# Attention: scores one pair earlier, two heads per VectorE step, and the softmax sums as a diagonal operand of a matrix product

## The reference

```
k_all = concat([k, k_ctx]); v_all = concat([v, v_ctx])       # 256 + 256 keys
s = einsum('bqkgd,bskd->bkgqs', q, k_all) * HEAD_DIM**-0.5   # 8 heads of 64
p = softmax(s, axis=-1)
o = einsum('bkgqs,bskd->bqkgd', p, v_all)
```

## Time and profile before

| | us |
|---|---|
| median of 3 runs | 3051.02 (3049.09 to 3054.16) |
| the profiled execution | 3051.58 |
| its span, first to last instruction | 3049.9 |
| TensorE busy | 2901.1 (95%) |
| VectorE busy | 1690.8 (55%) |
| ScalarE busy | 1332.0 (44%) |
| GpSimd busy | 204.1 (7%) |
| mean granted TensorE clock | 0.981 of full speed |

### The profile page before, as it was taken

The page is one execution under the profiler, slowest core; times in us unless marked ns, Lnnn a source line. Parts: engine busy times, 40 slices in busy tenths (PEclk is TensorE's granted clock), DMA queues, the critical chain, the costliest instruction groups (busy, mean ns, idle before and its releaser), DMA issues. The chain is left out here.

```text
span 3049.9 us, 49455 instructions
## 1 busy us (share of the span) xinstructions
PE 2901.1 (95%) x18122; PEld 2565.0 (84%) x18122; DVE 1690.8 (55%) x2279; ACT 1332.0 (44%) x1862; POOL 204.1 (7%) x224
## 2 busy tenths in 40 slices
PE   6999999889999999999987998899999999998998
PEld 5878887667888878888877998899999999998998
DVE  6444326646454244442276547875557486659864
ACT  5333315344343133432245445554645345545553
POOL 1000001200000000000020001300300000003100
PEclk7999999899999999999999999999999999999999
DMA  6444324113454225442233553355535556553454
GB/s 217 160 151 166 117 96 154 63 42 125 151 165 145 97 70 171 158 138 97 93 102 116 185 192 131 118 170 195 178 121 191 193 175 214 195 172 104 162 196 132
DMA packets 120490, 443.60 MB, mean 145 GB/s; under 512 B 13568, under 2 KB 14976, under 8 KB 119744
## 3 DMA queue, kind: packets, MB, share of 16 engines
q1 hardware_dynamic: 119376, 431.38, 42.7%
q0 software_dynamic: 1008, 10.75, 0.9%
HBM read 441.03 MB, written 1.05 MB: 145 GB/s over the span
## 5 line engine op out<-in xcount | busy, mean ns | idle before, releaser
L1497 DVE TENSOR_TENSOR wlo<-raw,whi 128x1024 fp32r<-128x1024 f32 x816 | 1001.1, 1240 | 922.7 <-ACT whi L1039 911.9
L1039 ACT ACTIVATE whi<-raw 128x1024 fp32r<-128x1024 f32 x816 | 848.6, 1054 | 941.0 <-PE ps L421 918.9
L419 PE MATMUL ps<-nh,whi 128*128 128x512 f32 (+1 forms) x1696 | 625.4, 369 | 20.1 <-DVE nl L1562 17.3
L420 PE MATMUL ps<-nl,whi 128*128 128x512 f32 (+1 forms) x1696 | 620.3, 366 | 0.0
L421 PE MATMUL ps<-nh,wlo 128*128 128x512 f32 (+1 forms) x1696 | 619.8, 365 | 0.0
L419 PE MATMUL ps<-bh,whi 128*128 128x256 f32 x1664 | 478.3, 287 | 11.1 <-DVE bl L1584 8.0
L420 PE MATMUL ps<-bl,whi 128*128 128x256 f32 x1664 | 468.1, 281 | 0.0
L421 PE MATMUL ps<-bh,wlo 128*128 128x256 f32 x1664 | 467.7, 281 | 0.0
L419 PEld LDWEIGHTS ps<-nh,whi 128*128 128x128 f32 x1696 | 322.4, 190 | 83.7 <-issue 19.3
L421 PEld LDWEIGHTS ps<-nh,wlo 128*128 128x128 f32 x1696 | 322.0, 190 | 56.1
L420 PEld LDWEIGHTS ps<-nl,whi 128*128 128x128 f32 x1696 | 322.2, 190 | 54.1 <-issue 0.2
(11 more groups left out here) (216 smaller groups left out, 3305.7 us busy)
## 6 DMA issues: line engine op xcount, KB each, us to landing
raw<-stream SPq DMA_DIRECT2D x816, 512.0 KB, 3.3
gates_w<-gate_in POOLq DMA_DIRECT2D x2, 3328.0 KB, 13.1
cst<-cst_in POOLq DMA_DIRECT2D x2, 1280.0 KB, 5.9
X<-x_in SPq DMA_DIRECT2D x1, 2048.0 KB, 11.3
out<-X SPq DMA_DIRECT2D x8, 128.0 KB, 2.0
fftw<-fftw_in POOLq DMA_DIRECT2D x2, 256.0 KB, 5.9
ws<-ws_in POOLq DMA_DIRECT2D x1, 512.0 KB, 3.9
poolw<-poolw_in POOLq DMA_DIRECT2D x2, 128.0 KB, 5.7
```

The costliest lines, as they stand in the source:

```text
L419: pe.matmul(dst, w1, rhs_hi, start=start, stop=False)
L420: pe.matmul(dst, w1, rhs_lo, start=False, stop=False)
L1039: act.activation(whi[:, r, :], raw[:, r, :], ACT.Copy).then_inc(w_hi_ready, 1)
L1497: dve.tensor_tensor(wlo[:, r, :], raw[:, r, :], whi[:, r, :].bitcast(F32), ALU.subtract).then_inc(w_ready, 1)
```

## The change

There are three edits, all in `attention`.

1. TensorE issues the scores of pairs 0 and 1 at the start, and those of pair p+2 in front of the odd unit's transposes of pair p. Before, the scores of pair p+1 stood in front of the even unit's transposes of pair p.
2. VectorE handles both units of a pair at once: one maximum over two PSUM banks, one product for the two `snm`, one reciprocal of two sums. It raises `nmax_ready` by two behind both, and waits for both scores and both exponentials.
3. `prob` is no longer scaled. VectorE writes `diag = ident * srs` (128 x 128 per unit), and TensorE computes `prob.T @ diag` as an ordinary f32 product where it transposed `prob` against `ident`. `diag` lies in free scratch space.

```diff
+        diag = sb("diag", [P, 4, P])
...
                 scores(0)
+                scores(1)
                 for u in range(n):
-                    if u % 2 == 0 and u + 2 < n:
-                        scores(u // 2 + 1)
+                    if u % 2 and u + 3 < n:
+                        scores(u // 2 + 2)
 
                     if u >= 2:
                         pe.wait_ge(pts_ready, c["att"] + u - 1)
-                    pe.wait_ge(prob_ready, c["att"] + u + 1)
+                    pe.wait_ge(scale_ready, c["att"] + u + 1)
                     kts = units[u][5]
                     for j in range(len(kts)):
-                        last = pe.transpose(ps[:, 2 + u % 2, j * P:(j + 1) * P],
-                                            prob[:, u % 4, j * P:(j + 1) * P], ident[:])
+                        last = pe.matmul(ps[:, 2 + u % 2, j * P:(j + 1) * P],
+                                         prob[:, u % 4, j * P:(j + 1) * P], diag[:, u % 4, :],
+                                         start=True, stop=True)
...
-                def normalise(u):
-                    nk = len(units[u][5]) * P
-                    dve.wait_ge(exp_ready, c["att"] + u + 1)
-                    link(dve.reciprocal(srs[:, u:u + 1], ssm[:, u:u + 1]))
-                    dve.tensor_scalar(prob[:, u % 4, 0:nk], prob[:, u % 4, 0:nk], srs[:, u:u + 1], None,
-                                      ALU.mult).then_inc(prob_ready, 1)
+                def normalise(pair):
+                    both = slice(2 * pair, 2 * pair + 2)
+                    dve.wait_ge(exp_ready, c["att"] + 2 * pair + 2)
+                    link(dve.reciprocal(srs[:, both], ssm[:, both]))
+                    for u in range(2 * pair, 2 * pair + 2):
+                        dve.tensor_scalar(diag[:, u % 4, :], ident[:], srs[:, u:u + 1], None,
+                                          ALU.mult).then_inc(scale_ready, 1)
...
-                for u, (g, s, t, h2, qt, kts) in enumerate(units):
+                for pair in range(n // 2):
+                    g, s, t, _, qt, kts = units[2 * pair]
                     nk = len(kts) * P
-                    q = qcol(l, t, s, qt, h2)
-                    dve.wait_ge(s_done, c["att"] + u + 1)
-                    link(dve.tensor_reduce(smx[:, u:u + 1], ps[:, S_BANK[u % 4], 0:nk], AX.X, ALU.max))
-                    dve.tensor_scalar(snm[:, u:u + 1], smx[:, u:u + 1], qscale[:, 1, q:q + 1], None,
-                                      ALU.mult).then_inc(nmax_ready, 1)
-                    if u:
-                        normalise(u - 1)
-                    if u >= 7 and u % 4 == 3:
-                        o_lower(u // 4 - 1)
-                normalise(n - 1)
+                    q = qcol(l, t, s, qt, 0)
+                    both = slice(2 * pair, 2 * pair + 2)
+                    b = S_BANK[2 * pair % 4]
+                    dve.wait_ge(s_done, c["att"] + 2 * pair + 2)
+                    link(dve.tensor_reduce(smx[:, both], ps[:, b:b + 2, 0:nk], AX.X, ALU.max))
+                    dve.tensor_tensor(snm[:, both], smx[:, both], qscale[:, 1, q:q + 2],
+                                      ALU.mult).then_inc(nmax_ready, 2)
+                    if pair:
+                        normalise(pair - 1)
+                    if pair >= 3 and pair % 2:
+                        o_lower(pair // 2 - 1)
+                normalise(n // 2 - 1)
                 o_lower(n // 4 - 1)
```

More of the change, by code:

```diff
@@ L297, in build @@
         exp_ready = sem("exp_ready")
-        prob_ready = sem("prob_ready")
+        scale_ready = sem("scale_ready")
         pt_done = sem("pt_done")
```

## The result

The changed kernel takes 3085.35 us (median of 4 runs, 3079.79 to 3090.70) beside 3050.06 us for the kernel before on the same chip (4 runs, 3046.49 to 3054.16). The ratio is 1.0115, with a 95% interval of 1.0092 to 1.0138. The forecast was 3075 with a range of 3057 to 3093: the direction and the range held, the size was too small, +24.3 against +35.3.

What follows compares the result with a forecast made beforehand. It took the two attention stages, with TensorE, VectorE and ScalarE in series, as bounding the span: +16.3 us in layer 0 and +8.0 in layer 1, +24.3 in total, gave 3075 us, range 3057 to 3093.

Steps and rivals of the forecast that it cites:

- The stall in the queue: Attention loop, even pairs from pair 4: reduction queued behind VectorE's output step, TensorE idle 2.9 us, 7.03 us a pair.
- The rival in which the queue doesn't decide: VectorE's output step finds the values done, only the product's price is left: 3052, no change; chance 0.05.
- Odd pairs: Attention loop: 4.19 us a pair against 4.42, the removed wait of 1.12 coming back as two products of 0.48.
- The price of the product: TensorE's f32 product replacing transposes: 0.22 us each, 1.05 for four against 0.57.
- the cheap and the dear product: Rivals on four products' price: 0.57 us like transposes, 3058, chance 0.07; or 1.83 us, 3103, chance 0.04.
- The layers at full clock: Attention stages summed at full clock: 77.2 us in layer 0 and 46.0 us in layer 1.
- The clock: Layer 0: one stretch at granted clock 0.50, kept from the kernel before and priced at 3.3 us.
- the clock falls again: Rival, TensorE's ten longer waits: each fall about 3 us, four give 3087, all ten 3105; chance 0.17.
- Faster: Rival, wait before odd transposes gone and nothing in its place: stages 53.0 and 34.1 us, -12, 3039; chance 0.05.

Runs made afterwards that it cites:

- experiment 1: Changed kernel with both steps on a group's output (ScalarE's copy, VectorE's subtraction) one pair later; 3056.56 us, ratio 1.0009.
- experiment 4: Kernel before with scores in front and the product with the diagonal, VectorE still one head a step; 3046.13 us, ratio 0.9989.
- experiment 9: Changed kernel with only VectorE's subtraction on the output one pair later, ScalarE's copy left in place; 3071.23 us, ratio 1.0059.
- experiment 6: Changed kernel with ten idle products in TensorE's wait before each even head's product from unit 6 on; 3077.42 us, ratio 1.0084.
- experiment 5: Kernel before with only the diagonal and f32 product in place of scaling and transpose, one head a step; 3056.82 us, ratio 1.0020.
- experiment 3: Kernel before with only the next scores moved in front of the odd transposes; 3041.35 us, ratio 0.9970.
- experiment 2: Changed kernel with transposes and in-place scaling again, scores in front and two heads a step kept; 3082.66 us, ratio 1.0099.
- experiment 8: Kernel before with only two heads per VectorE step, scores in the old place, transposes and in-place scaling; 3107.46 us, ratio 1.0182.
- experiment 11: Kernel before with scores in front, both output steps two units later, seven idle products in each layer's first TensorE wait; 3026.19 us, ratio 0.9911.

## Why the prediction was right, and where it was too small

**The stall in the queue: right.** The forecast had the reduction of an even pair queued behind L1763, that behind L1219, that behind the values, with TensorE idle for 2.9 us and 7.03 us for the pair. Measured in layer 1 are 2.83, and 7.13 and 7.17 from product to product. L1763 was to wait 3.7 to 4.6 us. Where a reduction stands behind it, it waits 4.7 and 5.8 us in layer 1 and 3.9 to 5.9 in layer 0, the longest around stretches at 0.50; the reduction follows with no wait for TensorE. Experiments 1, 4 and 9 show that this chain is the cause, and 4 that it takes the pairs to make it one. The rival in which the queue doesn't decide falls.

**Odd pairs: right within 0.1 to 0.5.** Forecast 4.19; measured in layer 1 4.33, 4.67 and 4.30, and 7.18 for the one pair that ran mostly at 0.50 (1641.73 to 1648.91 above). The wait before the products went and came back as work, as the step said. The start took 4.91 against 5.01.

**The price of the product: right.** Eight records come in 1.05 to 1.09 us against 1.05, so both the cheap and the dear product fall. The reduction of two heads was 1.22 as forecast, a diagonal 0.284 against 0.29.

**The layers at full clock: probably right.** This can't be read off the changed kernel itself, whose clock never stayed up. With its waits filled (experiment 6) the stages are 79.4 and 48.4 us at clocks of 0.98 and 0.96, against 77.2 and 46.0 in the forecast's addition at 1.00.

**The clock: the term that was mis-sized.** The step "It follows a part in which TensorE mostly waited, and the new start waits more, so I leave it in, at 3.3" priced one fall, in layer 0. There were six more in layer 0 and one in layer 1. The stages measure 14.0 and 3.4 us above the addition at full clock, 17.4 where 3.3 stood. TensorE's own rows give the same from another side. Experiments 5 and 4 have the same records as the changed kernel at a clock of 1.00 (512 in layer 0, busy 54.8 us; 321 in layer 1, busy 33.7); the changed kernel is busy 69.3 and 36.7, which is 14.5 and 3.0 more. The two ways, 17.4 and 17.5, agree, so about 14.1 us of the 38.6 are the clock's beyond the forecast, some 2 us for each of the seven falls that had no price. By medians the gap is 11.0; the profiled execution was the slowest of the four runs and had the lowest mean clock (0.973 beside 0.976 to 0.980), so the 14.1 may be more than a usual execution has.

The rival "the clock falls again" got 0.17 and the argument that layer 1 had waits and stayed at 1.00. That argument came from waits of at most 1.8 us and was carried over to waits of 2.8. The forecast and this rival were no alternatives: the stall makes the waits, and the waits make the clock fall. They should have been one case with one sum. The rival's 3087 for four falls is two us from the measured median by luck: seven more fell than the forecast had, at 2 us each and not 3.

**Faster: wrong as a whole, right in a part.** The rival had the wait before the odd transposes as a gain of 12 us if nothing takes its place. Experiment 3 takes this gain, 11.3 us. Two heads a step turn it round: they add 39.8 us to it (experiments 2 and 3), the product 6.6 (experiments 4 and 3).

## What to carry to other kernels

When an instruction is moved ahead on one engine, read on every other engine what stands in its queue between the old event and the new one: a small bookkeeping step that was free now waits for the part that was moved back, and holds up the critical chain behind it. Merging two tiles into one operation saves an engine's work but makes the chain two tiles long, and that pays only if the engine, not the chain, is the bound. Price the waits of TensorE with the slower clock that can come behind them, and add such a cost to the forecast that causes the wait, not to a rival.

## What the runs showed of the hardware

- At the end of waits of 2.3 to 2.9 us or shortly behind them the granted clock fell to 0.50 and stayed there for 3 to 7 us, with each of seven such waits in layer 0 of the changed kernel and with one of three in layer 1. The wait of 1.76 us at the start of the loop had a fall behind it in layer 0 of the kernel before, and none in layer 1. The length of the wait doesn't decide alone: the first wait of layer 1 is 2.91 us in the changed kernel and in experiments 1 and 6, and the clock fell behind it in these two only; it is 1.55 and 1.56 us in experiments 5 and 4, and the clock fell in 5 only. What decides is open.
- Less work beside waits at the same places gave a lower clock: 0.75 in experiment 2 against 0.81 in the changed kernel, and 0.62 in experiment 8, whose waits of 1.6 to 2.3 us are shorter but stand before every pair. So an operation that was made cheaper gave back less than its price (10.1 us for 13.1). These kernels also have transposes where the changed one has products, and the runs don't tell less work from another kind of work as the reason.
- Idle products in the wait raised the clock to 0.98 and 0.96 (experiment 6) and to 1.00 and 1.00 (experiment 11).
- Open also: the parts outside attention, which have the same instructions in all these kernels, differ between profiled executions (the first scores start anywhere from 580.4 to 586.4 us), so a single execution doesn't show a difference of a few us; the stages and the medians do.
